# A two-layer encoder on one core: the first weight panel loaded in three pieces between the tiles of x, and the rows of experts 0 and 1 selected and transposed by the same matrix products

## The reference

```python
def rmsnorm(x, g):
    y = xf * lax.rsqrt(jnp.mean(xf * xf, axis=-1, keepdims=True) + RMS_EPS) * g.astype(jnp.float32)
...
    proj = h @ w_in                       # attention: (512, 1024) @ (1024, 1536), h = rmsnorm(x)
...
    g_prob, g_idx = lax.top_k(jax.nn.softmax(g_logits, axis=-1), 1)
    e_prob, e_idx = lax.top_k(jax.nn.softmax(e_sel, axis=-1), TOP_K)
    hid = jax.nn.silu(jnp.einsum('td,edf->tef', t, w_gate)) * jnp.einsum('td,edf->tef', t, w_up)
    hid = hid * combine[..., None].astype(hid.dtype)
    return jnp.einsum('tef,efd->td', hid, w_down).reshape(B, S, D)
```

## Time and profile before

| | |
|---|---|
| median of three runs | 1280.29 us (1276.42 to 1282.89) |
| the profiled execution, its own time | 1278.82 us |
| its span in the profile | 1277.1 us |
| TensorE busy (matmul) | 1145.1 us, 90% |
| VectorE, ScalarE, GpSimd busy | 519.5, 383.5, 385.5 us |
| chain that ended last | PE 69%, DMA 13%, DVE 8%, ACT 4%, SPq 3% |
| largest DMA queue, SP's | 255.89 MB, 52.7% of 16 engines' span |

### The profile page before, as it was taken

How to read it: one execution, slowest core, us unless ns; L and a number is a source line. 1 busy time by engine, 2 the same in 40 slices (tenths; PEclk the granted TensorE clock), 3 DMA queues, 4 the chain that set the end, 5 groups by cost and what they waited for, 6 DMA issues and landing times.

```text
span 1277.1 us, 21577 instructions
## 1 busy us (share of the span) xinstructions
PE 1145.1 (90%) x8755; PEld 805.1 (63%) x8755; DVE 519.5 (41%) x1188; ACT 383.5 (30%) x854; POOL 385.5 (30%) x428
## 2 busy tenths in 40 slices
PE   5999999899999884989889999889999899999782
PEld 4876678655555442868568887678888555555441
DVE  4466663411111114564684455753653411111114
ACT  3426841111111102354553445543422111111010
POOL 1233621112232211047545266542301022322110
PEclk9999999999999997989999999999999899999896
DMA  7121047999999998111000120002366999999996
GB/s 241 67 73 67 2 192 277 368 364 381 383 386 379 383 392 320 69 66 67 2 3 1 67 101 31 3 2 81 151 247 261 359 372 389 388 386 377 380 390 247
DMA packets 67795, 278.24 MB, mean 218 GB/s; under 512 B 16888, under 2 KB 16984, under 8 KB 43120
## 3 DMA queue, kind: packets, MB, share of 16 engines
q1 hardware_dynamic: 56480, 255.89, 52.7%
q0 software_dynamic: 11072, 20.43, 4.7%
q10 hardware_dynamic: 144, 0.52, 0.1%
HBM read 265.83 MB, written 27.26 MB: 230 GB/s over the span
## 4 chain that ended last, share of the span: by engine, by line
PE 69%; DMA 13%; DVE 8%; ACT 4%; SPq 3%; issue 2%; POOL 1%; DVEq 0%; POOLq 0%
PE bank L1132 14%; PE bank L150 9%; PE bank L152 8%; PE bank L151 8%; DMA hn<-in_moe_w_up 8%; PE bank L1141 6%; PE bank L1676 4%; PE bank L1124 3%; DMA x<-in_moe_w_up 3%; SPq L2382 2%; PE bank L541 2%; PE bank L550 1%; PE bank L575 1%; PE bank L389 1%; PE bank L298 1%
## 5 line engine op out<-in xcount | busy, mean ns | idle before, releaser
L1002 POOL DMA_INDIRECT y_rows<-arena,idx_i x64 | 64.5, 1008 | 350.0 <-DVE arena L1319 345.0
L1224 ACT ACTIVATE arena<-bank 128x128 f32<-128x128 f32 x64 | 17.7, 277 | 368.2 <-PE bank L1132 368.2
L1323 DVE TENSOR_TENSOR arena<-arena,bank 128x128 f32<-128x128 f32 x64 | 18.4, 287 | 259.2 <-ACT arena L1224 259.2
L152 PE MATMUL bank<-ring_r,ht_r 128*128 128x512 f32 x288 | 113.0, 392 | 0.0
L1132 PE MATMUL bank<-ring,arena 128*64 128x256 f32 x832 | 101.6, 396 | 7.7 <-DMA ring<-in_moe_w_up 6.7
L1319 DVE COPY arena<-bank 128x512 f32<-128x512 f32 x64 | 44.2, 691 | 144.2 <-PE bank L1141 144.2
L150 PE MATMUL bank<-ring_r,arena_r 128*128 128x512 f32 (+1 forms) x228 | 91.3, 401 | 6.1 <-DVE ring_r L174 5.4
L151 PE MATMUL bank<-ring_r,arena_r 128*128 128x512 f32 x224 | 87.8, 392 | 0.0
L1132 PEld LDWEIGHTS bank<-ring,arena 128*64 128x64 f32 x832 | 57.9, 136 | 42.7 <-DMA ring<-in_moe_w_up 7.7
L151 PE MATMUL bank<-ht_r,ring_r 128*128 128x512 f32 (+1 forms) x224 | 80.9, 361 | 0.0
L1124 PEld LDWEIGHTS bank<-ident,arena 64*128 64x128 f32 x512 | 61.3, 201 | 28.3 <-issue 25.1
(11 more groups left out here) (343 smaller groups left out, 2338.4 us busy)
## 6 DMA issues: line engine op xcount, KB each, us to landing
ring<-in_moe_w_gate SPq DMA_DIRECT2D x26, 1024.0 KB, 21.5
ring<-in_moe_w_up SPq DMA_DIRECT2D x26, 1024.0 KB, 25.3
arena<-in_moe_w_down SPq DMA_DIRECT2D x24, 1024.0 KB, 27.5
ring<-in_moe_w_down SPq DMA_DIRECT2D x24, 1024.0 KB, 26.9
ring<-in_gdn_w_in SPq DMA_DIRECT2D x8, 2048.0 KB, 8.0
arena<-in_moe_w_gate SPq DMA_DIRECT2D x10, 1024.0 KB, 19.4
arena<-in_moe_w_up SPq DMA_DIRECT2D x10, 1024.0 KB, 23.3
ht<-in_moe_w_gate SPq DMA_DIRECT2D x10, 1024.0 KB, 27.0
```

The source lines that it names most:

```text
L152: return pe.matmul(dst, a[1], b[0], start=False, stop=stop)
L1002: pool.indirect_dma_start(out=y_rows[l], out_offset=bass.IndirectOffsetOnAxis(ap=idx_i[:, 1, e:e + 1], axis=0), in_=y_out[:, e % RING, :], ...
```

## The change

It has two parts.

*Start.* SP issues x tile 0, chunks 0 and 1 of panel 0 (512 KB), x tile 1, chunks 2 and 3 (512 KB), chunks 4 to 7 (1024 KB), x tiles 2 and 3, and then panel 1 as before. Each piece of panel 0 has a semaphore of its own. On ScalarE the first split of panel 0 stands right behind the squares of tiles 0 and 1, and the squares of tiles 2 and 3 come after the whole split. On VectorE the first low split stands ahead of tile 1's scaling, and tiles 2 and 3 are scaled after the whole panel is split and tile 1's low part is written.

*MoE.* `pick_rows` now has `hn` as the operand that stays (128 rows by every eighth column, `hn[:, t, c::KC]`) and the matrix of zeros and ones as the moving one, 128 columns: 8 chunks times 4 tiles. What comes out is already transposed. ScalarE copies the first four chunks of expert 0 and then of expert 1 to `xgt` (256 columns each), VectorE the last four. `turn(0)` and `turn(1)` and their two copies of 512 columns are gone, and so are the copies to `xg`. The fetches for experts 4 and 5 no longer wait for them.

```diff
+        late_weights = [sem(f"late_weights{l}") for l in range(2)]
+        FIRST_IN = 16
+        FIRST = (late_weights[0], late_weights[1], panel_full[0])
...
         def split_high(act, n, quarters=range(4)):
             for q in quarters:
-                if q == 0:
+                if n == 0 and q < 3:
+                    act.wait_ge(FIRST[q], FIRST_IN)
+                elif q == 0:
                     act.wait_ge(panel_full[n % 2], 16 * (n // 2 + 1))
...
             def gather(e):
-                if e >= AHEAD:
-                    pool.wait_ge(s["turned"], e - AHEAD + 1 + l * PER["turned"])
+                if e >= AHEAD + EARLY:
+                    pool.wait_ge(s["turned"], e - AHEAD - EARLY + 1 + l * PER["turned"])
...
+        def picked(e, half):
+            return (xgt[:, e, half * 4 * SLOTS:(half + 1) * 4 * SLOTS].rearrange("p (c n) -> p c n", c=4),
+                    pick_bank(half).rearrange("p (c n) -> p c n", c=4)[:, :, e * SLOTS:(e + 1) * SLOTS])
...
-                for t in range(TT):
-                    for half in range(2):
-                        last = pe.matmul(pick_bank(half)[:, :], picks[0][:, t, :], hn[:, t, half * HALF:(half + 1) * HALF],
+                for c in range(KC):
+                    for t in range(TT):
+                        last = pe.matmul(pick_bank(c // 4)[:, c % 4 * P:(c % 4 + 1) * P], hn[:, t, c::KC], picks[0][:, t, :],
                                          start=t == 0, stop=t == TT - 1)
...
                 pe.wait_ge(s["xgt"], e + 1 + l * PER["xgt"])
+                if e < EARLY:
+                    pe.wait_ge(pick["kept"], PICK["kept"] + EARLY * l + e + 1)
                 gate_and_up(e % RING, slot).then_inc(s["up"], 1)
-                if e < EXPERTS - 1:
+                if EARLY <= e + 1 < EXPERTS:
                     turn(e + 1)
...
             pick_rows()
-            turn(0)
...
             act.wait_ge(pick["rows"], PICK["rows"] + 1 + l)
-            act.copy(xg[:, 0, 0:HALF], pick_bank(0)[:, :]).then_inc(pick["kept"], 1)
+            for e in range(EARLY):
+                act.copy(*picked(e, 0)).then_inc(s["xgt"], 1)
...
-            take(0)
...
             dve.wait_ge(pick["rows"], PICK["rows"] + 1 + l)
-            dve.tensor_copy(xg[:, 0, HALF:D], pick_bank(1)[:, :]).then_inc(pick["kept"], 1)
+            for e in range(EARLY):
+                dve.tensor_copy(*picked(e, 1)).then_inc(pick["kept"], 1)
...
+            first = rows(ap["attn_w_in"][0])[:, :, IN_ORDER[0] * PANEL:(IN_ORDER[0] + 1) * PANEL]
+            load_x(0)
+            for q, (signal, chunks) in enumerate(zip(FIRST, (slice(0, 2), slice(2, 4), slice(4, KC)))):
+                sp.dma_start(panel(0)[:, chunks, :], first[:, chunks, :]).then_inc(signal, 16)
+                if q == 0:
+                    load_x(1)
+            for t in (2, 3):
+                load_x(t)
...
-            for t in range(TT):
+            for t in range(2):
                 act.wait_ge(x_in[t], 16)
                 square_rows(act, t)
+            split_high(act, 0, (0,))
             turn_act(act, 0, 0)
-            split_high(act, 0, (0,))
+            split_high(act, 0, (1,))
             turn_act(act, 0, 1)
-            split_high(act, 0, (1, 2, 3))
+            split_high(act, 0, (2, 3))
+            for t in (2, 3):
+                act.wait_ge(x_in[t], 16)
+                square_rows(act, t)
...
             norm_dve(dve, 0, 0)
+            split_low(dve, 0, (0,))
             norm_dve(dve, 0, 1)
             turn_dve(dve, 0, 0)
-            split_low(dve, 0, (0,))
+            split_low(dve, 0, (1, 2, 3))
+            turn_dve(dve, 0, 1)
             norm_dve(dve, 0, 2)
-            split_low(dve, 0, (1,))
-            turn_dve(dve, 0, 1)
-            split_low(dve, 0, (2, 3))
             norm_dve(dve, 0, 3)
             turn_dve(dve, 0, 2)
             turn_dve(dve, 0, 3)
```

More of the change, by code:

```diff
@@ L926, in build @@
         late_dma = [sem(f"late_dma{l}") for l in range(2)]
-        late_weights = [sem(f"late_weights{l}") for l in range(2)]
         late_step = [sem(f"late_step{l}") for l in range(2)]
@@ L930, in build @@
                    ranks=1, pos=1, placed=2 * TT, lists=1, idx=1, combined=TT)
-        PER.update({n: EXPERTS for n in ("st", "turned", "xgt", "up", "silu", "hidden", "hid_turned", "hid_t",
+        PER.update(turned=EXPERTS - EARLY)
+        PER.update({n: EXPERTS for n in ("st", "xgt", "up", "silu", "hidden", "hid_turned", "hid_t",
                                          "y_sum", "y_copied")})
@@ L1075, in after @@
                             if weights:
-                                eng.wait_ge(late_weights[l], eng.compute_val((k + 1) * LATE_WEIGHTS))
+                                eng.wait_ge(late_weights[l], eng.compute_val(FIRST_IN + (k + 1) * LATE_WEIGHTS))
                                 return
@@ L1086, in late_passes @@
                 eng.wait_ge(late_dma[l], LATE * LATE_DMA)
-                eng.wait_ge(late_weights[l], LATE * LATE_WEIGHTS)
+                eng.wait_ge(late_weights[l], FIRST_IN + LATE * LATE_WEIGHTS)
         def spare_pe(pe, n, b):
@@ L1156, in turn @@
             def turn(e):
-                if e < EARLY:
-                    pe.wait_ge(pick["kept"], PICK["kept"] + 2 * (l + 1))
-                else:
-                    pe.wait_ge(xg_full[e % AHEAD], rows_in(l, e))
-                if e:
+                pe.wait_ge(xg_full[e % AHEAD], rows_in(l, e))
+                if e > EARLY:
                     pe.wait_ge(s["xgt"], e + l * PER["xgt"])
@@ L2457, in _, with load_x @@
         def _(sp):
-            for t in range(TT):
+            def load_x(t):
                 sp.dma_start(x[:, t, :], ap["x"][0, t * P:(t + 1) * P, :]).then_inc(x_in[t], 16)
+            first = rows(ap["attn_w_in"][0])[:, :, IN_ORDER[0] * PANEL:(IN_ORDER[0] + 1) * PANEL]
[6 more added lines that the diff above has]
+                load_x(t)
             for i, j in enumerate(IN_ORDER):
-                load_panel(sp, i, rows(ap["attn_w_in"][0])[:, :, j * PANEL:(j + 1) * PANEL],
-                           (a["proj"], 4) if i == 2 else None)
+                if i:
+                    load_panel(sp, i, rows(ap["attn_w_in"][0])[:, :, j * PANEL:(j + 1) * PANEL],
+                               (a["proj"], 4) if i == 2 else None)
                 if i == 1:
```

3 lines of the change are left out of this document (1 added, 2 removed).

## The result

The changed kernel is slower: 1289.17 us, the median of 6 runs (1287.55 to 1293.1), against 1279.03 us for the kernel before (6 runs, 1276.42 to 1282.89). The ratio is 1.0075, with an interval of 1.0057 to 1.0094. The forecast was 1271.2 us with a range up to 1277.0. It went the way of the rival "the weight loads are not hidden", which had a chance of 0.07, half of it at 1294.6 and half at 1280.5; the measured time lies between the two.

What follows compares the result with a forecast made beforehand. Each MoE stage was taken to end with its stream of expert loads, the earlier part being mostly TensorE's work. Gains 2.3 + 3.2 + 2.9 = 8.4 us off 1278.8 gave 1270.4 (1271.9 by the median); 1271.2 was taken, range 1267.5 to 1277.

Steps and rivals of the forecast that it cites:

- the weight loads are not hidden: Rival, chance 0.07: in `pick_rows` each load and product cost 0.30 us, 12.4 us more per layer, whole 1294.6 us.
- part 2: The MoE in each layer: load streams end 3.2 us earlier in layer 0 and 2.9 in layer 1.
- The stride costs nothing there.: Strided loads in the transposes of x take 193 ns yet come about 0.11 us apart; `pick_rows` was expected likewise.
- 0.3 longer: `pick_rows`, per layer: 64 records with own weight loads, 0.111 us apart, take 7.3 us instead of 7.03.
- the border of 0.175: In `pick_rows`: above 0.11 + 0.065 us per record, 64 records twice eat the 8.4 us gain.
- its second case: `pick_rows` loads end to end at 0.193 us without the product: 12.4 us, whole 1280.5; half of the rival's 0.07.
- The price of a hole: Time lost in load-stream gaps around expert 0, reckoned against 424 GB/s: 6.5 us in layer 0, 5.7 in layer 1.
- holes two and three: Load-stream gaps before expert 0's `gate_and_up` ends and while expert 1's place is awaited: together 3.5 and 3.2 us.
- the start: Part 1: first product at 16.85, tile 2's transposes at 24.3 instead of 26.65, 2.3 us earlier, passed on in full.
- The way behind T: From the end of `pick_rows` to expert 0: one copy and two hand-overs, 0.6 us instead of 2.6.
- The clock that stays up: After the shorter pause, expert 0's `gate_and_up` runs in the full clock: 3.8 us instead of 5.44.
- a stage ends with its loads: A MoE stage ends when its load stream ends, earlier only if that starts earlier or has fewer holes.

Runs made afterwards that it cites:

- e5_readstep: Changed kernel, but VectorE's scaling ahead of each MoE reads every eighth column and writes neighbours, so `hn`'s readers there take neighbouring columns: 1274.65 us, ratio 0.9959.
- e10_narrow8: Changed kernel with each 128-column product of `pick_rows` made as two of 64, each with its own step-of-eight weight load: 1324.54 us, one run.
- e11_narrow1: Changed kernel with each `pick_rows` product made as two of 64 columns, with neighbouring columns as weights: 1286.92 us, one run.
- e3_contiguous: Changed kernel with `pick_rows` taking 128 neighbouring columns of `hn` as weights instead of every eighth (experts 0 and 1 see another column order): 1275.43 us, ratio 0.9958.
- e1_start: Kernel before with only the new order at the start, its MoE left as it was: 1278.73 us, ratio 0.9985.
- e8_step2: Changed kernel with `pick_rows` taking every second column of `hn` as weights instead of every eighth: 1276.0 us, one run.
- e6_writestep: Like e5_readstep, but VectorE reads neighbouring columns and writes them at a distance of 128 columns: 1274.66 us, ratio 0.9971.
- e7_twice: Like e3_contiguous, but every product of `pick_rows` made twice: 1288.69 us, ratio 1.0077.
- e9_step4: Changed kernel with `pick_rows` taking every fourth column of `hn` as weights instead of every eighth: 1287.32 us, one run.

## Why the prediction was wrong

**The step that failed** is in part 2: "The stride costs nothing there." The term it carried, "0.3 longer", was 8.5 and 8.2 us. The transposes of x have stepped loads 0.11 apart, and I took this spacing over to full-precision products. Two things were overlooked, and both stood in the trace of before. One is the duration. I read 193 ns and compared it with nothing; transposes of neighbouring columns of the same `hn`, in attention, are there as well (groups by form, the kernel before):

```profile
L606 PEld LDWEIGHTS bank<-ident,hn 128*128 128x128 f32 x32 | 3.5, 141 | 0.8 <-issue 0.7
```

141 ns against 193: the step did cost 52 ns a load. The other is who sets the pace. Transposes of 128 columns are 0.109 and 0.110 us apart (medians of L606 and L298), stepped or not, so a stepped load that could start every 0.11 us is hidden in them. The transposes of the experts' rows have stepped loads too (64 rows by 128 columns), send 64 columns behind each and still take 1.09 us for eight. Half the columns in the same time means that the load sets the pace there. `e5_readstep`, where these columns lie together, shows it, first before, then in `e5_readstep` (timeline, one expert's eight transposes):

```profile
271.30 1.09 PE L1124 MATMUL bank<-ident,arena 64*128 64x64 f32 x8
```

```profile
271.64 0.71 PE L1140 MATMUL bank<-ident,arena 64*128 64x64 f32 x8
```

Within them the median from one load to the next falls from 0.110 to 0.062 us. So a step of 8 about doubles the time between loads in both kinds: from 0.06 or less to 0.11 for a transpose (at 0.06 the product may set the pace), 0.11 to 0.24 for a full-precision product. I had seen each half of it, the stepped transposes and the products with neighbouring columns, each at 0.11, and concluded that the combination would be 0.11 too. Two factors of two were in play, and each row showed only one of them.

**The rival** had the right place, the loads inside `pick_rows`, and the wrong working. "Each pair costs 0.193 + 0.111 = 0.30 us" adds product to load. The measured 0.238 is above the border of 0.175 that it named, but it is no sum: `e10_narrow8` and `e11_narrow1` halve the product and leave the spacing. Nearer is its second case, loads without the product, but it put them end to end at 0.193: here a load takes 0.335 and they are 0.238 apart, so they overlap one another. The rule of the Trainium skill (TensorE: Matmul & The Clock Gate, Part 3, The mechanism), that a load overlaps a running product only in another group of rows, would give that 0.30. The sign came out as it said, but not its reason: with neighbouring columns, loads of 0.192 us over the whole array are 0.112 apart. The trace speaks against the rule, as the prediction had it; what was missed lay elsewhere.

**The price of a hole** was too high, by the prediction's own rows. I reckoned holes two and three at the full 424 GB/s, 3.5 and 3.2 us. The rate of the stage as a whole is 388. Against that they are 18 x (1 - 272/388) = 5.4, less 4 x (1 - 111/388) = 2.9, which makes 2.5 us, and by the same working 2.2 in layer 1. The terms would have been 2.2 and 1.9 instead of 3.2 and 2.9, and the whole 6.4 us instead of 8.4. `e3_contiguous` has the `pick_rows` of the forecast and gained 2.6 to 8.3 us; that holds 6.4, and 8.4 lies just outside. From the start of `pick_rows` to the last expert, in us, one execution each:

| | layer 0 | layer 1 |
|---|---|---|
| MoE of before: before, `e1_start` | 239.9, 240.5 | 241.4, 239.3 |
| `pick_rows` of 7.3 to 7.7 us: `e3_contiguous`, `e8_step2`, `e5_readstep`, `e6_writestep` | 237.7, 237.9, 237.9, 238.0 | 241.4, 238.8, 238.9, 238.8 |

In layer 0 every pair gives 1.9 to 2.9 us of gain. In layer 1 the spread within each row, up to 2.6 us, is as large as the gain, perhaps in part because the clock of the old MoE fell in one execution and not in the other. So the lower price is an estimate that fits the runs, and not one that they measure.

**Right**, point by point: the start (16.65 and 24.22 against 16.85 and 24.3; 2.1 of the 2.3 us are there at the first `pick_rows`, and what is left of them at the end is not shown). One reading in it is not covered by the clock rows: it calls products 0.42 us apart "slow clock", while the granted clock of that stretch is given as 1.00 at both spacings. The way behind T, 0.61 us. The clock that stays up, 3.85 us for `gate_and_up` (in layer 1 of `e1_start` it stayed up without the change). The closed holes. That a stage ends with its loads: the queue's wait for `pick_rows` grew by what `pick_rows` grew by, and `e7_twice` reproduced the loss, within its interval, by length alone.

**Open**: single executions scatter, by 3.1 us ahead of the first `pick_rows` and by 5.1 between the layers in the eight traces named above, where their programs are the same. Why a stepped load is slow, and why the jump lies between 8 and 16 bytes, no run shows. Steps other than 1, 2, 4 and 8, and loads of a narrower type, were not tried.

## What to carry to other kernels

When a cost is taken over from a row of another form, ask what sets the pace in that row: a spacing is the larger of two times and hides the smaller. Look for a pair of rows that differ only in the property in question (here neighbouring and stepped loads), and for the row where the cover is thinnest (here 64 columns instead of 128). Then, a layout that one operand's reader wants is best made where the data is written anyway, on an engine that has time: it cost VectorE 0.9 us a tile, and that kernel gained 3.2 to 7.3 us, while the same sorting in the weight loads cost 8 us a layer on the path. And a gain of one or two microseconds read from a single pair of traces should be held against a second trace of the unchanged part: here that took most of layer 1's gain away.

## What was not expected of the hardware

- The weight load has a rate of its own. For full-precision 128 x 128 weights it is one per 0.112 us at step 1, 0.118 at step 2, 0.233 at step 4 and 0.238 at step 8. For transposes it is at most 0.062 at step 1 and 0.110 at step 8. At a granted clock of 0.50 it was the same 0.235 as at 1.00.
- VectorE slows down as well: scaling 128 x 1024 float32 takes 1.28 us, with two operands read at step 8 (22.8 - 4 x 1.285)/8 = 2.2 us, and with the result written at a distance of 128 columns (21.6 - 5.1)/8 = 2.1. The groups by form, x12 with four of the plain kind among them, of `e5_readstep`:

```profile
L298 DVE SCALAR_TENSOR_TENSOR hn<-x,norm_s,gain 128x1024 f32<-128x1024 f32 x12 | 22.8, 1897 | 8.2 <-POOL norm_s L282 8.2
```

and of `e6_writestep`:

```profile
L298 DVE SCALAR_TENSOR_TENSOR hn<-x,norm_s,gain 128x1024 f32<-128x1024 f32 x12 | 21.6, 1797 | 8.2 <-POOL norm_s L282 8.2
```

- The clock fell from 1.00 to 0.50 in `e10_narrow8` while TensorE was never idle by its records: all it did there were loads 0.238 us apart and products of 64 columns. In `e9_step4` and `e11_narrow1` the clock was 1.00 all through the picking.
- Behind the same two pauses of 0.8 us the clock fell in layer 1 of the kernel before (0.65 in its stretch) and not in layer 1 of `e1_start` (1.00).
